# Two attention blocks on one core: the second block's token-wise products regrouped to 512 columns, and the heads' scaling put on GpSimd

## The reference, cut to what matters

```python
def hybrid_layer(x, mem, norm_g, w_in, w_out, mem_norm_g, w_mem_kv, qk_g):
    h = rms_norm(x, norm_g)
    proj = jnp.einsum('btd,de->bte', h, w_in)
    sizes = [D_MOBA] * 4 + [D_DIL] * 4 + [D_MEM] * 2        # 384 x 8, 256 x 2
    a_q, a_k, a_v, a_g, b_q, b_k, b_v, b_g, m_q, m_g = jnp.split(proj, cuts, axis=-1)
    ...
```

## Time and profile before

| what | value |
|---|---|
| median of three runs | 1619.04 us |
| the profiled execution, its own time | 1618.99 us |
| its span, first to last instruction | 1617.2 us |
| busy: TensorE, weight loads, VectorE, ScalarE, GpSimd | 98%, 81%, 57%, 47%, 3% |
| mean granted clock of TensorE | 0.998 of 2.4 GHz |
| block 2, layer 0: aq to the end of av | 1051.7 to 1139.9 us |
| DMA, share of 16 engines | 26% |

### The profile page before, as it was taken

One profiled execution on the slowest core, in us unless ns is written; L12 is line 12 of the kernel. 1 busy time (PEld: TensorE's weight loads), 2 busy tenths in 40 slices (PEclk: granted clock), 3 DMA queues, 4 the chain that ended last, 5 costly groups with the idle time before them and its releaser, 6 DMA issues.

```text
span 1617.2 us, 22039 instructions
## 1 busy us (share of the span) xinstructions
PE 1577.1 (98%) x8345; PEld 1309.0 (81%) x8345; DVE 920.8 (57%) x1940; ACT 755.3 (47%) x1587; POOL 46.3 (3%) x75
## 2 busy tenths in 40 slices
PE   6999999999999999999999999999999999999999
PEld 6887777788887887777778888799877779987777
DVE  4597546443354469655544434639856554985663
ACT  5443544433333353545333323534666644556672
POOL 0000001000001000000200000100000010000000
PEclk9999999999999999999999999999999999999999
DMA  6222112233323322211232334233121233312121
GB/s 222 88 79 90 53 40 79 92 91 92 103 80 97 98 92 91 67 52 54 79 91 91 92 104 126 83 98 89 57 65 47 79 98 105 91 56 70 40 79 65
DMA packets 80885, 136.07 MB, mean 84 GB/s; under 512 B 8190, under 2 KB 33548, under 8 KB 80780
## 3 DMA queue, kind: packets, MB, share of 16 engines
q1 hardware_dynamic: 77120, 129.22, 26.2%
q10 hardware_dynamic: 3660, 5.44, 1.1%
HBM read 132.55 MB, written 2.10 MB: 83 GB/s over the span
## 4 chain that ended last, share of the span: by engine, by line
PE 87%; DVE 9%; ACT 2%; issue 1%; DMA 0%; ACTq 0%; POOL 0%; DVEq 0%
PE gemm_bank L726 71%; PE aux_bank L852 3%; PE aux_bank L831 3%; PE aux_bank L796 2%; PE aux_bank L812 2%; PE aux_bank L781 1%; DVE w_lo L1470 1%; PE aux_bank L757 1%; PE aux_bank L840 1%; DVE probs L1631 1%; DVE rope L1572 1%; PE aux_bank L697 1%; PE aux_bank L1015 1%; PE aux_bank L750 0%; PE aux_bank L906 0%
## 5 line engine op out<-in xcount | busy, mean ns | idle before, releaser
L1105 ACT ACTIVATE w_hi<-raw 128x512 fp32r<-128x512 f32 (+3 forms) x524 | 305.2, 587 | 621.4 <-PE gemm_bank L726 620.7
L1470 DVE TENSOR_TENSOR w_lo<-raw,w_hi 128x512 fp32r<-128x512 f32 (+3 forms) x524 | 329.8, 635 | 414.3 <-ACT w_hi L1105 413.0
L726 PE MATMUL gemm_bank<-act_hi,w_hi 128*128 128x512 f32 x768 | 310.9, 405 | 6.2 <-ACT mq_flat L1143 2.9
L726 PE MATMUL gemm_bank<-act_hi,w_lo 128*128 128x512 f32 x768 | 299.7, 390 | 0.0
L726 PE MATMUL gemm_bank<-act_lo,w_hi 128*128 128x512 f32 x768 | 299.5, 390 | 0.0
L726 PE MATMUL gemm_bank<-w_hi,act_hi 128*128 128x384 f32 (+3 forms) x736 | 266.3, 362 | 1.1 <-DVE qk_c L1510 1.1
L726 PE MATMUL gemm_bank<-w_lo,act_hi 128*128 128x384 f32 (+3 forms) x736 | 257.2, 349 | 0.0
L726 PE MATMUL gemm_bank<-w_hi,act_lo 128*128 128x384 f32 (+3 forms) x736 | 257.2, 349 | 0.0
L726 PEld LDWEIGHTS gemm_bank<-act_hi,w_hi 128*128 128x128 f32 x768 | 144.3, 188 | 43.4 <-issue 11.1
L726 PEld LDWEIGHTS gemm_bank<-act_hi,w_lo 128*128 128x128 f32 x768 | 144.2, 188 | 31.0
L726 PEld LDWEIGHTS gemm_bank<-act_lo,w_hi 128*128 128x128 f32 x768 | 144.5, 188 | 28.6 <-issue 1.0
(11 more groups left out here) (303 smaller groups left out, 2097.6 us busy)
## 6 DMA issues: line engine op xcount, KB each, us to landing
raw<-in_w_in SPq DMA_DIRECT2D x104, 512.0 KB, 3.4
raw<-in_w_in SPq DMA_DIRECT2D x64, 384.0 KB, 3.3
raw<-in_w_out SPq DMA_DIRECT2D x32, 512.0 KB, 3.6
raw<-in_w_branch SPq DMA_DIRECT2D x24, 512.0 KB, 3.6
raw<-in_w_mem_kv SPq DMA_DIRECT2D x8, 512.0 KB, 3.7
raw<-in_w_in SPq DMA_DIRECT2D x16, 256.0 KB, 2.7
raw<-in_w_in SPq DMA_DIRECT2D x8, 416.0 KB, 4.8
x<-in_x SPq DMA_DIRECT2D x4, 512.0 KB, 5.2
```

The source lines that it names most:

```text
L726: last = pe.matmul(o, a, c, start=begin and n == 0, stop=end and n == 2)
L1105: act.activation(w_hi[:, s % RING, 0:n], raw[:, p % RAW, kk % PIECE, 0:n], ACT.Copy)\
L1470: dve.tensor_tensor(w_lo[:, s % RING, 0:n], raw[:, p % RAW, kk % PIECE, 0:n], w_hi[:, s % RING, 0:n].bitcast(F32), ALU.subtract).then_inc( ...
```

## The change

The seven token-wise groups (six of 384 columns, one of 256) become five of 512, cut without regard to what the columns make: t0 = aq and ak[0:128], t1 = ak[128:384] and bq[0:256], t2 = bq[256:384] and bk, t3 = av and bv[0:128], t4 = bv[128:384] and mq. A step loads two stretches of columns by two DMAs. ScalarE copies every bank, by two instructions each; VectorE's copy of ak goes. The attention's filling begins with t4 in place of bv and mq. The a heads are now laid beside t2 alone, three parts to a step, and beside the first steps of t3; the led events stand one step later. And the eight multiplications of head tiles by their roots leave VectorE (a and b heads, not the memory's): VectorE signals that the roots are there, GpSimd multiplies the tiles one after the other, and VectorE waits for the four q tiles before it rotates q and for the four k tiles before it rotates k.

```diff
+TOKEN_FEATURES = [("aq", 0, WA), ("ak", WA, WA), ("bq", 4 * WA, WB), ("bk", 4 * WA + WB, WB),
+                  ("av", 2 * WA, WA), ("bv", 4 * WA + 2 * WB, WB), ("mq", 4 * WA + 4 * WB, WE)]
+def token_groups():
+    out, at = [[]], 0
+    for what, c0, n in TOKEN_FEATURES:
+        done = 0
+        while done < n:
+            if at == T:
+                out.append([])
+                at = 0
+            m = min(n - done, T - at)
+            out[-1].append((what, done, at, c0 + done, m))
+            at, done = at + m, done + m
+    return out
...
+        for tag, segments in TOKENS.items():
+            def tokens(k0, k1, segments=segments, l=l):
+                return [(at, w["w_in_2"][l, k0 * P:k1 * P, c:c + m]) for _, _, at, c, m in segments]
+            add((2, l, tag), tokens, KD, T, 4)
...
-        fill = [((2, l, g), KD) for g in ("bv", "mq", "ag", "bg", "mg")] + [((2, l, "out", 0), EARLY)]
+        fill = [((2, l, g), KD) for g in ("t4", "ag", "bg", "mg")] + [((2, l, "out", 0), EARLY)]
-        a.lead = {2: [("turn", 0, 0)], 3: [("low", 0, 0)], 4: [("scores", 0)], 5: [("scores", 2)], 6: [("scores", 3)]}
+        a.lead = {3: [("turn", 0, 0)], 4: [("low", 0, 0)], 5: [("scores", 0)], 6: [("scores", 2)], 7: [("scores", 3)]}
...  # ScalarE, block 2
+            def evict_tokens(name):
+                gi = gi_of(2, l, name)
+                for b in range(NT):
+                    wait_gemm_full(act, gi, b)
+                    for what, c, at, _, m in TOKENS[name]:
+                        ins = act.activation(flat_2(what)[:, b, c:c + m], gemm_bank[b][:, at:at + m], ACT.Copy)
+                    ins.then_inc(gemm_read[b], 1)
...  # ScalarE: the squares of the b heads wait for step 4 of t3; then, after the led steps
+            for event in a.lead[KD - 1]:
+                exponentials(a, event[1])
+            split.through(gi)
+            evict_tokens("t3")
...  # VectorE, head_norm, behind the roots
+            if pool_tiles is not None:
+                dve.engine_nop().then_inc(head_roots_ready, 1)
+                for _ in range(4):
+                    yield
+                dve.wait_ge(head_tiles_scaled, pool_tiles)
+                return
...  # VectorE, block 2
-            alongside(a_heads, [gi_of(2, l, n) for n in ("bq", "bk")], 2)
+            alongside(a_heads, [gi_of(2, l, "t2")], 3, drain=False)
             for kk in range(KD):
...
-                for _ in range(2):
+                for _ in range(3 if kk < 2 else 0):
+                    next(a_heads, None)
+                for _ in a_heads if kk == 2 else ():
+                    pass
+                for _ in range(2 if kk > 3 else 0):
                     next(b_heads, None)
-                split.beside(gi_of(2, l, "av"), kk)
+                split.beside(gi_of(2, l, "t3"), kk)
...  # GpSimd, block 2
+            for n, a in enumerate("ab"):
+                pool.wait_ge(head_roots_ready, 2 * l + n + 1)
+                for i, (what, t) in enumerate(itertools.product("qk", range(NT))):
+                    tile = kinds[a + what][:, t, :, :]
+                    r = head_rstd[:, i * AH:(i + 1) * AH].unsqueeze(2).to_broadcast([P, AH, HD])
+                    pool.tensor_tensor(tile, tile, r, ALU.mult).then_inc(head_tiles_scaled, 1)
```

More of the change, by code:

```diff
@@ L57 @@
 PIECE = 2
+TOKEN_FEATURES = [("aq", 0, WA), ("ak", WA, WA), ("bq", 4 * WA, WB), ("bk", 4 * WA + WB, WB),
[12 more added lines that the diff above has]
+    return out
+TOKENS = {f"t{i}": segments for i, segments in enumerate(token_groups())}
 def constants():
@@ L1036, in block_2 @@
         def block_2(l):
-            gemm(gi_of(2, l, "aq"), "tokens", ready=part_ready((2, l, "x")))
-            for name in ("ak", "bq", "bk"):
+            gemm(gi_of(2, l, "t0"), "tokens", ready=part_ready((2, l, "x")))
+            for name in ("t1", "t2"):
                 gemm(gi_of(2, l, name), "tokens")
             a = attention_2(l)
-            gemm_led(gi_of(2, l, "av"), "tokens", a, lambda kk: None)
+            gemm_led(gi_of(2, l, "t3"), "tokens", a, lambda kk: None)
             y_ready = lambda kk: pe.wait_ge(y2_lo_ready, KD * l + kk + 1)
@@ L1381, in block_2 @@
         def block_2(l):
-            evict(gi_of(2, l, "aq"), ACT.Copy, lambda b: flat_2("aq")[:, b, :])
-            split.through(gi_of(2, l, "ak"))
+            def evict_tokens(name):
[5 more added lines that the diff above has]
+                    ins.then_inc(gemm_read[b], 1)
+            for name in ("t0", "t1"):
+                split.through(gi_of(2, l, name))
+                evict_tokens(name)
             def kind_tiles(a):
                 return [kinds[a + n][:, t, :, :] for n in ("q", "k") for t in range(NT)]
-            wait_gemm_read(act, gi_of(2, l, "aq"))
-            wait_gemm_read(act, gi_of(2, l, "ak"))
+            wait_gemm_read(act, gi_of(2, l, "t1"))
             for n, _ in enumerate(head_squares(kind_tiles("a"), sq_2)):
[L1391 to L1395, removed]
+                split.beside(gi_of(2, l, "t2"), n // 2)
+            split.through(gi_of(2, l, "t2"))
+            evict_tokens("t2")
+            wait_gemm_read(act, gi_of(2, l, "t2"))
             b_squares = head_squares(kind_tiles("b"), sq_2)
             a = attention_2(l)
-            gi = gi_of(2, l, "av")
+            gi = gi_of(2, l, "t3")
             for kk in range(KD):
-                for _ in range(2):
-                    next(b_squares, None)
+                if kk > 3:
+                    for _ in range(2):
+                        next(b_squares, None)
                 split.beside(gi, kk)
@@ L1512, in _, with head_norm @@
         head_tiles = [0]
-        def head_norm(tiles, fine=False):
+        def head_norm(tiles, fine=False, pool_tiles=None):
             c = 0
@@ L2055, in block_2 @@
             dve.wait_ge(causal_loaded, 16)
-            split.through(gi_of(2, l, "aq"))
-            evict(gi_of(2, l, "ak"), lambda b: flat_2("ak")[:, b, :])
+            split.through(gi_of(2, l, "t0"))
+            split.through(gi_of(2, l, "t1"))
             def kind_heads(a, gain):
                 qq, kk = kinds[a + "q"], kinds[a + "k"]
-                yield from head_norm([tile[:, t, :, :] for tile in (qq, kk) for t in range(NT)])
+                tiles = 2 * NT * (2 * l + "ab".index(a))
+                yield from head_norm([tile[:, t, :, :] for tile in (qq, kk) for t in range(NT)],
+                                     pool_tiles=tiles + NT)
                 for tile, g in ((qq, gain), (kk, gain + 1)):
+                    if tile is kk:
+                        dve.wait_ge(head_tiles_scaled, tiles + 2 * NT)
                     yield from rotate(tile, 0, HD // 2, gain_2[:, l, g, :], cos2[:, :, :], sin2[:, :, :],
```

26 lines of the change are left out of this document (10 added, 16 removed).

## The result

| what | before | after |
|---|---|---|
| median of five runs | 1619.04 us (1618.49 to 1619.75) | 1627.40 us (1624.51 to 1628.13) |
| ratio of after to before | | 1.0046, 95% interval 1.0034 to 1.0058 |
| profiled execution, span | 1618.99, 1617.2 us | 1624.94, 1623.1 us |
| busy: TensorE, VectorE, ScalarE, GpSimd | 98, 57, 47, 3% | 97, 56, 46, 5% |
| matmul starts in the trace | 8345 | 7961 |

What follows compares the result with a forecast made beforehand. TensorE bounds the kernel, a block-2 layer being a queue of matmuls almost without waits. Per layer -2.3 + 0.2 + 6.8 + 1.0 - 1.4 - 0.8 + 0.7 = +4.2; two, +8.4 on 1618.99, give 1627.4 us (range 1613 to 1633).

Steps and rivals of the forecast that it cites:

- Matmuls, -2.3: Token groups of block 2: 480 matmuls of 512 columns take 109.0 us in place of 111.3, 2.3 us less a layer.
- Loads and copies, 0.2: Loads and bank copies: loads cost nothing; copies wait behind the led scores' exponentials in front of t4, 0.2 us (0 to 1.5).
- The chain of the a heads, 31.75 against 28.8: First square to turn: 31.75 us of work where 28.8 are left, so TensorE waits 3.0 us a layer.
- Exclusion, 3.8: VectorE's rotation and GpSimd's k tiles exclude each other, adding 3.8 us a layer (0 to 5.0) to the a heads.
- the prediction's own sign: TensorE's wait for a heads or remainders: 6.8 us a layer if tiles and rotation exclude each other, 3.0 if not.
- The b heads, +1.0: In the attention, where VectorE has 4 us in 20 free: 1.0 us more a layer (0 to 4).
- Led waits, -1.4: Waits at the led events (0.8 and 0.6) go, since longer steps stand between them: 1.4 us less a layer.
- mq, -0.8: TensorE's 1.5 us wait for mq's copies shrinks by 0.8 us a layer (0 to 1.5).
- ag to bg, +0.7: In the attention, bg's second bank waits for the reading of ag's first: 0.7 us more a layer (0 to 1.5).
- Rival C: The forecast plus a clock fall in block 2, costing 3.4 us: one layer 1630.8, both 1634.2; chance 0.12.
- A: GpSimd works beside VectorE undisturbed: -0.6 us a layer, 1617.8 us; chance 0.26.
- B: Not slower, as the a heads' chain is not late: -3.8 us a layer, 1611.4 us; chance 0.12.

Runs made afterwards that it cites:

- experiment 3: Changed kernel, but VectorE makes q's four tables ahead of its wait for GpSimd's q tiles, for a and b heads: 1626.43 us, ratio 1.0046.
- The first experiment: Changed kernel, but VectorE multiplies the a and b head tiles by their roots, as before; the five groups stay: 1628.58 us, ratio 1.0057.
- experiments 6: Changed kernel with one number of the attention's filling rule changed (1.2 for 12 steps, not 1.3 for 13): 1625.12 us, ratio 1.0043.
- 8: Changed kernel with later turn, GpSimd for b tiles only, filling rule 1.2 for 12 steps, second pair turned an attention step later: 1618.09 us, ratio 0.9997.
- 9: Kernel of 8, plus aq's tables made early, three a-head squares a step, and t3 copied ahead of the last led scores' exponentials: 1616.51 us, ratio 0.9985.

## Why the prediction was right, and where it was not

The time was forecast as 1627.4 and is 1627.4. The cause holds (the a heads come late, GpSimd and VectorE exclude each other), but that the two numbers are equal is luck: the forecast had 4.2 us a layer and no fall of the clock, and the layers are 2.8 and 2.1 us longer, with the clock for most of the rest. For a layer, the steps as the prediction put them:

- **Matmuls, -2.3.** 480 token matmuls a layer, 0.227 us apart: right. What the layer's length leaves when waits and stops are taken off is -1.9 (2.8 longer, with 3.4 us more of waits and five more stops of 0.27), and by the same account -1.4 to -2.2 in the other regrouped kernels, -2.6 in the last.
- **Loads and copies, 0.2.** Right: 0.2 us of wait for t3's banks in layer 0, none for a load, in this trace.
- **The chain of the a heads, 31.75 against 28.8.** First square at 1095.94 (1096.5), sums 9.0 (9.0), roots 2.8 (2.85), a q tile 0.89 (0.95): right. Too dear were the remainders: there are six of 0.6 us, as forecast, but only four stood in the chain, since two ran while VectorE waited for GpSimd anyway. An engine's wait covers what is queued beside it, and I had added both: 1.2 us too much. The fourth is the one between the rotation's last sum and the signal for the turn. With the exclusion the forecast chain is 31.75 + 3.8 = 35.6 us long; from first square to turn it is 33.9.
- **Exclusion, 3.8.** The mechanism is right, by the tables' 3.45 for 0.94 and by experiment 3. It costs 2.5 here, and not the tiles' whole 3.3: beside instructions as small as these GpSimd's tiles were hardly held up (0.83 to 0.88 us each); why is not shown. The wait is 3.9 us, in four stops that cost some 1.0 more, in place of 6.8. By the prediction's own sign (6.8 us with exclusion, 3.0 without) 3.9 would point the wrong way; it is the length of the tables, and of the products in experiment 3, that decides.
- **The b heads, +1.0.** No wait for them. The first experiment shows what I had not asked: without GpSimd they are late, 1.8 us and a stop. The same edit costs in one place and pays in the other.
- **Led waits, -1.4.** Both went. But the 0.6 for k_lo stood at 1228 us, in the attention, not among the led events where the prediction put it.
- **mq, -0.8.** -1.2: it waits 0.3.
- **ag to bg, +0.7.** 1.7 in layer 0, 1.3 in layer 1, the largest error in a small term: gates of ag stand on VectorE behind two scores of 512 columns and the memory heads.
- **Not in the sum at all:** the 0.27 us of each stop (five more, 1.35), 0.3 for spread_inv, and the clock. Rival C had the fall but hung it on a wait of 6.8 us and priced it at 3.4. It came with 2.9, at 1.4, in the trace in one layer. The runs at a clock of 0.995 take 3 us more than those at 0.997, and 0.002 x 1625 = 3.3 us; so the median has about two falls of 3.4 us more than the profiled run. Where they are is not shown, since no trace of such a run of this kernel was taken; that of experiment 3 has 6.8 us at the lower level in block 1, as the kernel before, and a fall in both layers of block 2.

Rivals A and B fell: the tables' length rules out A, and the wait of 2.9 us at the turn B. For the 8.4 us, then: 2.8 + 2.1 for the longer layers, 1.4 for the fall in layer 1, -0.4 ahead of block 2, and 2.5 by which the median lies over the profiled run, most likely clock. Three things stay open: those 2.5 us; why layer 0 of the profiled run kept its clock through the same wait at which layer 1 lost it; and how much of the -1.4 to -2.6 us the matmuls bring, since stops too short for the list of waits are not counted in it.

## What to carry to other kernels

Work handed to an engine that holds up the giver while both run is not off the chain unless the giver has other things to do meanwhile: here GpSimd's tiles cost 1.1 us a layer on the a heads' chain and saved 1.8 in the attention, and leaving GpSimd only the tiles of the second place was worth 4 us, the clock included. Before an edit that moves the start of a chain, count the slack at its end in the profile (2.8 us here), and move the consumer with it; it was a small edit of the order, worth 5 us, about half of it clock. Price each new stop of TensorE above its idle time, and one of 3 us with a likely fall of the clock on top; and when a wait is mended, read what stood behind it, since in three runs here (experiments 6, 8 and 9) part of what was mended stood at another place.

## What was not expected of the hardware

- A stop of the stream of 512-column matmuls costs 0.27 us beyond the wait that the profile names (0.16 before the first start, 0.11 before the second); where transposes or scores follow it is 0.16 to 0.22.
- In the traces of block 2 a fall of the clock came with waits of 1.7, 2.9, 3.5 and 3.7 us, with each of 3.5 or more, with four of the six of 2.9, with one of the five of 1.7 to 1.8, and never with one of 1.5 or less; the clock was at 1.2 GHz for 3.4 or 6.8 us, of which up to 0.9 lay inside the wait.
- GpSimd multiplies a 128x384 tile by a broadcast factor in 0.83 us. Beside VectorE's 128x128 tables it takes 0.83 to 0.88 while they take 0.91 for 0.29. Where VectorE's 128x512 remainders and 128x768 products stand beside it, it takes 1.38 on average, a remainder 1.3 for 0.69 and a product 1.6 for 0.95.
